# A first input tile in three column groups, and a burst of constant matmuls ahead of it

## The chip, the cores and the metric

The kernel runs on one core of a Trainium2 chip. The metric is the device time of one execution in microseconds; the figure given for a kernel is the median of several runs. Engines are named PE (matmul), ACT, DVE and POOL (element-wise work), and SP, which issues the DMAs here. Each engine works through its own list of instructions in order and meets the others only at semaphores.

## The reference

One step of a one-layer hybrid decoder: 1024 prompt rows and 8 sample rows of width 1024. What matters for the change is the head of it:

```
h = RMSNorm(x, g_pre)            # (1032, 1024)
z = h @ w_in                     # 1024 -> 2432 columns, split among three groups
u, v, ga, xb, gb, q, gc = split(z)
```

Group A is a chunked spatial gate on u and v, group B a short convolution and a gated linear recurrence, group C a cross attention into 256 memory rows. Their outputs are concatenated, multiplied with w_out, normalised and added to x. All of it is float32.

## The kernel before

**Layout.** x is kept transposed: 8 k-tiles of 128 features, each 128 partitions by 1032 columns (1024 prompt rows and 8 sample rows). The columns are worked on in NG = 3 groups of GN = 344. The input projection runs over 19 weight tiles of 128 outputs (m = 0 to 18), each of 8 k-tiles.

**Three products for one.** Each float32 product is made of three matmuls on rounded parts. ACT rounds a tile (x_hi, for x together with the factor g_pre; w_hi), DVE or POOL subtracts the rounded part from the whole (x_lo, w_lo), and `parts` (L358 to L364) multiplies w_hi with x_hi, w_hi with x_lo and w_lo with x_hi. So one k-tile of one weight tile is 9 matmuls, three for each column group. The norm's factor is applied later, on the results, since it is a factor per column; its sum of squares is made from the same tiles by ACT (L684) and DVE (L1042).

**The order at the start.** SP issues, all on one hardware queue (L255 to L262): the parameters, the first 256 columns of weight tile 0, k-tile 0 of x (L262), the rest of weight tile 0 (L259), k-tile 1, weight tile 1 (L246), k-tiles 2 to 7. Each load of a k-tile has a semaphore of its own (xT_in). ACT waits for each (L680), rounds it (L681) and counts xhi_done; DVE waits for that (L1037), makes x_lo (L1038) and counts xlo_done. ACT's and DVE's roundings and splits of weight tile 0 and 1 stand between those of k-tiles 0, 1 and 2 (L672, L677, L664; L1027).

PE's `start_tiles(m, k)` does the 9 matmuls of one k-tile for weight tile 0 or 1 and waits for the k-tile once, ahead of its first matmul. The opening order on PE is: tile 0 with k-tiles 0, 1, 2, then tile 1 with k-tile 0, tile 0 with k-tiles 3 and 4, and so on. Results of tiles 0 and 1 lie in PSUM banks 0 to 5. The tile `ones` (128x128), which POOL sets early (L922), is used on PE for the sum of squares over partitions (L407); PSUM bank 7 is first used there too.

**After the start.** ACT's rounding of weight tile 2 waits for the end of tile 0 on PE; behind it stand the rest of the squares, the sums on DVE, the memory projection and the reciprocal root, which PE waits for before the rest of tile 2 and 3.

Of the kernel before, what the change touches and what calls it, by code (L numbers as in the profile page):

```python
# [26 lines left out]
F = mybir.dt.float32  # L27
R = mybir.dt.float32r
ALU = mybir.AluOpType
ACT = mybir.ActivationFunctionType  # L30
AX = mybir.AxisListType

P = 128
# [3 lines left out]
KT = DM // P  # L37
NG = 3
GN = TT // NG
# [16 lines left out]
for _name, _n in (("g_pre", 8), ("g_mem", 8), ("w_conv", 12), ("b_conv", 3), ("b_a", 3), ("b_x", 3),  # L56
                  ("lam", 3), ("st_conv", 72), ("st_h", 24), ("b_s", 4)):
    PAR[_name] = _at
    _at += _n
N_PAR = _at  # L60

K_ORDER = [3, 4, 5, 6, 7, 0, 1, 2]
MIX_BANKS = (6, 7, 4)
# [24 lines left out]
def build(nc, d):  # L88
    with ExitStack() as ctx:
# [3 lines left out]
        def sem(name):  # L93
            return ctx.enter_context(nc.semaphore(name))

        x_hi, x_lo = sb("x_hi", [P, KT, TT], R), sb("x_lo", [P, KT, TT], R)
# [9 lines left out]
        ident, ones = sb("ident", [P, P]), sb("ones", [P, P])  # L106
# [12 lines left out]
        ps = ctx.enter_context(nc.psum_tensor("ps", [P, 8, 512], F))  # L119
# [58 lines left out]
        def wo_source(n):  # L178

            if n in (0, 1, 7):  # L180
                return w_stage[:, n % 7, :]
            return wo_early[:, n - 2, :] if n < 6 else zT[:, 0, 0:DM]

        def pc(name, i=0, n=1):
            return par[:, PAR[name] + i:PAR[name] + i + n]
# [3 lines left out]
            "par_in", "rows_in", "gatew_in", "wsT_in", "memn_in"))  # L189
        memT_in = [sem(f"memT_in{i}") for i in range(4)]  # L190
        wm_in = [sem(f"wm_in{i}") for i in range(4)]
        xT_in = [sem(f"xT_in{k}") for k in range(KT)]
        w_in = [sem(f"w_in{i}") for i in range(2)]
        x_in = [sem(f"x_in{i}") for i in range(2)]
        c_in = [sem(f"cache_in{i}") for i in range(6)]
        wo_in = [sem(f"wo_in{i}") for i in range(KT)]
        gpost_in = sem("gpost_in")
        y_stored = [sem(f"y_stored{i}") for i in range(2)]
        kv_stored, conv_stored, h_stored, vs_stored, ys_stored = map(sem, (
            "kv_stored", "conv_stored", "h_stored", "vs_stored", "ys_stored"))  # L200
        const_set, w_masked, wlo_done, qc_done, xsq_done, whi_done, xhi_done = map(sem, (
            "const_set", "w_masked", "wlo_done", "qc_done", "xsq_done", "whi_done", "xhi_done"))
        xlo_done, memg_done, ms_done, root_done, xsum_done, rstdB_done = map(sem, (
            "xlo_done", "memg_done", "ms_done", "root_done", "xsum_done", "rstdB_done"))
# [39 lines left out]
        def _(sp):  # L244
# [9 lines left out]

            sp.dma_start(par[:, :], d["par"]).then_inc(par_in, 16)  # L255
            sp.dma_start(w_stage[:, 0, 0:WF], d["w_tiles"][0, :, 0:WF]).then_inc(wfirst_in, 16)
            for k in range(KT):
                if k == 1:
                    sp.dma_start(w_stage[:, 0, WF:DM], d["w_tiles"][0, :, WF:DM]).then_inc(w_in[0], 16)  # L259
                if k == 2:  # L260
                    load_w(1, 1)
                sp.dma_start(mixT[:, k, :], d["xT"][:, k, :]).then_inc(xT_in[k], 16)  # L262
            sp.wait_ge(wlo_done, 1)
            load_w(2, 0)
            for i in range(4):
# [38 lines left out]
            sp.wait_ge(a_done, 9)  # L304

            def load_wo(n):
                sp.dma_start(wo_source(n), d["w_out"][K_ORDER[n]]).then_inc(wo_in[n], 16)

            for n in range(2, 6):
                load_wo(n)  # L310
# [46 lines left out]
        def _(pe):  # L357
            def parts(g, slot, k, cols, x, bank):  # L358

                wk = slice(k * P, (k + 1) * P)  # L360
                for n, (w, xx) in enumerate(((w_hi, x_hi), (w_hi, x_lo), (w_lo, x_hi))):
                    last = pe.matmul(ps[:, bank, 0:GN], w[:, slot, wk], xx[:, k, cols],  # L362
                                     start=(x == 0 and n == 0), stop=(x == KT - 1 and n == 2))
                return last  # L364
# [18 lines left out]
            def start_tiles(m, k):  # L383
                if m == 0 and k == 0:
                    pe.wait_ge(wfirstlo_done, 1)
                elif (m, k) in ((0, WF // P), (1, 0)):
                    pe.wait_ge(wlo_done, m + 1)
                if m == 0:
                    pe.wait_ge(xlo_done, k + 1)
                for g in range(NG):  # L390
                    last = parts(g, m, k, slice(g * GN, (g + 1) * GN), k, 3 * m + g)
                    if k == KT - 1:
                        last.then_inc(z_done, 1)

            for k in range(KT):
                start_tiles(0, k)
                if k in (2, 4, 6):
                    start_tiles(1, k // 2 - 1)
# [7 lines left out]
            for g in range(NG):  # L406
                pe.matmul(ps[:, 5 + g, 0:GN], ones[:, :], probs[:, g * GN:(g + 1) * GN],  # L407
                          start=True, stop=True).then_inc(rstdp_done, 1)
# [3 lines left out]
            for k in range(KT):  # L412
                pe.wait_ge(mlo_done, k // 2 + 1)
                pe.wait_ge(wmlo_done, k // 2 + 1)
                for mt in range(MT):
                    for n, (a, w) in enumerate(((memT_hi, w_mem_hi), (memT_lo, w_mem_hi),
                                                (memT_hi, w_mem_lo))):
                        last = pe.matmul(ps[:, 3 + mt, :], a[:, k, mt * P:(mt + 1) * P], w[:, k, :],
                                         start=(k == 0 and n == 0), stop=(k == KT - 1 and n == 2))
# [16 lines left out]
            with pe.Fori(0, 4) as i:  # L436
                for u in range(2):
                    m, s = i * 2 + (ATT0 + u), i * 2 + u
                    pe.wait_ge(qc_done, s * 2 + 2)
                    for t in range(2):  # L440
                        for hh in range(2):
# [4 lines left out]
                                             start=False, stop=True)  # L446
# [10 lines left out]
                    for h in range(NH):  # L457
                        if h % 2 == 0:
                            pe.wait_ge(pTlo_done, s * 2 + (h // 2 + 1))
                        for mt in range(MT):  # L460
                            pT = slice((2 * h + mt) * P, (2 * h + mt + 1) * P)
                            pe.matmul(ps[:, 7, h * 2 * HD:(h + 1) * 2 * HD], probsT_hi[:, pT], v_hl[:, mt, h, :],  # L462
                                      start=(mt == 0), stop=(mt == 1), skip_group_check=True)
# [171 lines left out]
            for x, k in enumerate(K_ORDER):  # L635
                for n in range(2):
                    cols = slice(n * 512, (n + 1) * 512)
                    pe.matmul(ps[0:2 * NL, 6 + n, :], o_s[:, k, :], wo_hi[:, k, cols],
                              start=(x == 0), stop=(x == KT - 1), skip_group_check=True)
                    last = pe.matmul(ps[0:NL, 6 + n, :], o_s[:, k, 0:NL], wo_lo[:, k, cols],  # L640
                                     start=False, stop=(x == KT - 1), skip_group_check=True)
# [14 lines left out]
        def _(act):  # L656
# [14 lines left out]
            act.wait_ge(wfirst_in, 16)  # L671
            act.activation(w_hi[:, 0, 0:WF], w_stage[:, 0, 0:WF], ACT.Copy).then_inc(wfirsthi_done, 1)  # L672
            act.wait_ge(par_in, 16)
            for k in range(KT):
                if k == 1:
                    act.wait_ge(w_in[0], 16)
                    act.activation(w_hi[:, 0, WF:DM], w_stage[:, 0, WF:DM], ACT.Copy).then_inc(whi_done, 1)  # L677
                if k == 2:
                    split_tile(1)
                act.wait_ge(xT_in[k], 16)  # L680
                act.activation(x_hi[:, k, :], mixT[:, k, :], ACT.Copy, scale=pc("g_pre", k)).then_inc(xhi_done, 1)  # L681
            for k in range(KT):
                act.wait_ge(xlo_done, k + 1)
                act.activation(mixT[:, k, :], mixT[:, k, :], ACT.Square).then_inc(xsq_done, 1)  # L684
                if k == 3:
                    split_tile(2)
# [182 lines left out]
            split_o(0, 1)  # L869

            for n, k in enumerate(K_ORDER):
                act.wait_ge(wo_in[n], 16)
                if n < KT - 1:
                    act.wait_ge(x_free, n + 1)
                else:
                    act.wait_ge(z_done, 3 * N_TILES)
                act.activation(wo_hi[:, k, 0:DM], wo_source(n), ACT.Copy).then_inc(wohi_done, 1)
# [127 lines left out]
        def _(dve):  # L1005
# [12 lines left out]
            def grp(g):  # L1018
                return slice(g * GN, (g + 1) * GN)
# [10 lines left out]
            dve.wait_ge(wfirsthi_done, 1)  # L1030
            low_w(0, slice(0, WF)).then_inc(wfirstlo_done, 1)

            for k in range(KT):
                if k in (1, 2):
                    dve.wait_ge(whi_done, k)
                    low_w(k - 1, slice(WF, DM) if k == 1 else slice(0, DM)).then_inc(wlo_done, 1)
                dve.wait_ge(xhi_done, k + 1)  # L1037
                dve.scalar_tensor_tensor(x_lo[:, k, :], mixT[:, k, :], pc("g_pre", k), x_hi[:, k, :].bitcast(F),  # L1038
                                         ALU.mult, ALU.subtract).then_inc(xlo_done, 1)
            for k in range(1, KT):  # L1040
# [215 lines left out]
            for g in range(NG):  # L1256
                evac(15, g, zT[:, 10, grp(g)])
                for c in range(3 * g, 3 * g + 3):
                    dve.wait_ge(mT_done, c + 1)
                    n, a = (P, 0) if c < NCH else (NS, P - NS)  # L1260
# [175 lines left out]
```

## Time and profile before

| | us |
|---|---|
| runs | 455.29, 454.79, 454.98 |
| median | 454.98 |
| span of the profiled execution | 450.6 |
| own time of the profiled execution | not recorded beyond its span |
| median less span | 4.4 |
| PE busy | 428.5 |
| DVE busy | 230.0 |
| ACT busy | 172.9 |
| POOL busy | 133.2 |

The span runs from the first to the last instruction of the profiled execution. Busy times are sums of instruction times; the ends of matmuls are modelled, so one matmul's time overlaps the next one's. Starts, and the step from one start to the next, are the surer readings.

### The profile page before, as it was taken

Reading aid. Unit: us, or ns where it says so; the run is one execution under the profiler, and the core shown is the slowest. Engines: PE = TensorE matmul, PEld = TensorE weight load, DVE = VectorE, ACT = ScalarE, POOL = GpSimd, SP = SyncE. Lnnn points to the kernel's source line nnn. Section 1 sums busy time; section 2 is a strip of 40 time slices with the busy share of each in tenths; the row PEclk is TensorE's granted clock in tenths of the full one; section 3 lists DMA queues with packets and bytes.
Section 4 is the critical chain, followed back from the end, with each engine's and each line's share of the span. In section 5 each row is a group of like instructions: output and inputs, shape, how many; then the busy total and the mean of one; then the engine's idle time right before and its main releaser. Section 6 shows DMA issues by size and latency. Waiting matters only on the chain.

```text
span 450.6 us, 6211 instructions
## 1 busy us (share of the span) xinstructions
PE 428.5 (95%) x2452; PEld 375.7 (83%) x2452; DVE 230.0 (51%) x325; ACT 172.9 (38%) x284; POOL 133.2 (30%) x71
## 2 busy tenths in 40 slices
PE   2999979999999999999999879999999999999994
PEld 2999878999999999998889577887899768888883
DVE  4978898333476674334359933265465634111112
ACT  5963655232232232225482330743725432222211
POOL 0024812132142232112039820410502323444440
PEclk9999999999999999999999969999999999999998
DMA  8990010111011111011042410132215320222222
GB/s 294 384 412 21 31 64 9 41 47 47 0 47 49 49 47 47 0 47 48 0 153 81 140 49 1 47 125 109 63 36 153 93 94 0 93 93 93 93 97 93
DMA packets 12916, 38.18 MB, mean 85 GB/s; under 512 B 2096, under 2 KB 2488, under 8 KB 12768
## 3 DMA queue, kind: packets, MB, share of 16 engines
q1 hardware_dynamic: 12896, 37.91, 24.2%
q8 instruction: 13, 0.21, 0.2%
q14 instruction: 7, 0.06, 0.0%
HBM read 33.07 MB, written 4.83 MB: 84 GB/s over the span
## 4 chain that ended last, share of the span: by engine, by line
PE 80%; DVE 11%; ACT 3%; issue 3%; DMA 2%; SPq 1%; DVEq 0%; ACTq 0%
PE ps L362 40%; PE ps L627 20%; PE ps L491 2%; PE ps L486 2%; PE ps L445 2%; PE ps L462 2%; PE ps L444 2%; DMA mixT<-in_xT 2%; PE ps L453 2%; PE ps L561 1%; PE ps L539 1%; DVE zT L1224 1%; DVE probs L1042 1%; DVE memT_lo L1057 1%; PE ps L464 1%
## 5 line engine op out<-in xcount | busy, mean ns | idle before, releaser
L362 PE MATMUL ps<-x_hi,w_hi 128*128 128x344 f32 x456 | 152.2, 334 | 11.4 <-DVE x_lo L1038 8.9
L362 PE MATMUL ps<-x_hi,w_lo 128*128 128x344 f32 x456 | 146.9, 322 | 0.0
L362 PE MATMUL ps<-x_lo,w_hi 128*128 128x344 f32 x456 | 146.8, 322 | 0.0
L362 PEld LDWEIGHTS ps<-x_hi,w_hi 128*128 128x128 f32 x456 | 87.1, 191 | 15.4 <-issue 14.3
L914 POOL TENSOR_TENSOR w_lo<-w_stage,w_hi 128x1024 fp32r<-128x1024 f32 x17 | 40.7, 2392 | 173.2 <-ACT w_hi L664 173.2
L362 PEld LDWEIGHTS ps<-x_lo,w_hi 128*128 128x128 f32 x456 | 87.0, 191 | 0.1
L362 PEld LDWEIGHTS ps<-x_hi,w_lo 128*128 128x128 f32 x456 | 86.8, 190 | 0.0
L627 PE MATMUL ps<-x_hi,w_hi 128*128 128x512 f32 x128 | 50.6, 395 | 0.0
L627 PE MATMUL ps<-x_hi,w_lo 128*128 128x512 f32 x128 | 50.5, 394 | 0.0
L627 PE MATMUL ps<-x_lo,w_hi 128*128 128x512 f32 x128 | 50.5, 394 | 0.0
L664 ACT ACTIVATE w_hi<-w_stage 128x1024 fp32r<-128x1024 f32 x18 | 19.0, 1054 | 69.0 <-PE ps L362 68.9
L1011 DVE TENSOR_TENSOR zT<-ps,rstdB 128x344 f32<-128x344 f32 (+1 forms) x27 | 13.8, 513 | 46.1 <-PE ps L362 46.1
L987 POOL TENSOR_TENSOR zT<-zT,x_ring 128x1024 f32<-128x1024 f32 x7 | 16.8, 2396 | 42.5 <-DVE zT L1323 42.5
L627 PEld LDWEIGHTS ps<-x_hi,w_lo 128*128 128x128 f32 x128 | 24.1, 188 | 5.7
L627 PEld LDWEIGHTS ps<-x_hi,w_hi 128*128 128x128 f32 x128 | 24.0, 188 | 5.7
L627 PEld LDWEIGHTS ps<-x_lo,w_hi 128*128 128x128 f32 x128 | 24.0, 188 | 5.7
L1318 DVE TENSOR_SCALAR sy<-sy 128x1 f32<-128x1 f32 x7 | 1.1, 154 | 54.2 <-ACT probs L860 54.2
L944 POOL TENSOR_TENSOR q_st<-zT,q_st 64x256 fp32r<-64x256 f32 x16 | 14.0, 875 | 45.7 <-ACT q_st L716 44.3
L860 ACT ACTIVATE probs<-ps 128x1024 f32<-128x1024 f32 x7 | 7.2, 1025 | 51.9 <-PE ps L627 51.9
L979 POOL TENSOR_TENSOR w_lo<-mixT,w_hi 128x1024 fp32r<-128x1024 f32 x8 | 19.2, 2398 | 21.2 <-ACT w_hi L852 21.2
L738 ACT ACTIVATE probs<-ps,negm 128x256 f32<-128x256 f32 x32 | 14.7, 473 | 18.8 <-DVE negm L1117 18.8
L1011 DVE TENSOR_TENSOR mixT<-ps,rstdB 128x344 f32<-128x344 f32 x15 | 7.4, 514 | 24.1 <-PE ps L362 24.0
(196 smaller groups left out, 662.4 us busy)
## 6 DMA issues: line engine op xcount, KB each, us to landing
w_stage<-in_w_tiles SPq DMA_DIRECT2D x18, 512.0 KB, 3.3
mixT<-in_xT SPq DMA_DIRECT2D x8, 516.0 KB, 7.9
x_ring<-in_x_all SPq DMA_DIRECT2D x8, 512.0 KB, 4.0
o_y<-zT SPq DMA_DIRECT2D x7, 512.0 KB, 2.9
zT<-in_w_out SPq DMA_DIRECT2D x5, 512.0 KB, 4.6
zT<-in_w_mem SPq DMA_DIRECT2D x4, 512.0 KB, 12.6
zT<-in_kcT SPq DMA_DIRECT2D x8, 256.0 KB, 4.1
zT<-in_vc SPq DMA_DIRECT2D x8, 256.0 KB, 6.1
```

What stands on the lines that cost most here:

```text
L362: last = pe.matmul(ps[:, bank, 0:GN], w[:, slot, wk], xx[:, k, cols], start=(x == 0 and n == 0), stop=(x == KT - 1 and n == 2))
L444: pe.matmul(out, q_st[:, u, hh, t, :], k_hh[:, hh, t, :], start=True, stop=False)
L445: last = pe.matmul(out, q_st[rows_h, u, hh, t, :], k_lo[rows_h, t, :], start=False, stop=True)
L453: last = pe.transpose(ps[:, 5 + b, n * P:(n + 1) * P], probs[:, (4 * b + n) * P:(4 * b + n + 1) * P], ident[:, :])
L627: last = pe.matmul(ps[:, 3 * u + n, :], o[:, u, ok], w[:, k, cols], start=(x == 0 and part == 0), stop=(x == KT - 1 and part == 2))
L664: act.activation(w_hi[:, slot, :], w_stage[:, slot, :], ACT.Copy).then_inc(whi_done, 1)
L738: act.activation(probs[:, h * NM:(h + 1) * NM], ps[:, 3 + hh, t * NM:(t + 1) * NM], ACT.Exp, bias=negm[:, n:n + 1], scale=HD ** -0.5, accu ...
L914: pool.tensor_tensor(w_lo[:, slot, :], w_stage[:, slot, :], w_hi[:, slot, :].bitcast(F), ALU.subtract).then_inc(wlo_done, 1)
L944: pool.tensor_tensor(q_st[to, u, hh, :, :], zT[r, 0:2, bass.ds(i * (2 * P) + u * P, P)], q_st[r, u, hh, :, :].bitcast(F), ALU.subtract).th ...
L979: pool.tensor_tensor(o_lo[:, slot, :].rearrange("p (k n) -> p k n", k=KT), mixT[:, :, bass.ds(c0, P)], o_hi[:, slot, :].bitcast(F).rearran ...
L987: pool.tensor_tensor(y_out[:, u, :], y_out[:, u, :], x_ring[:, u, 0:DM], ALU.add).then_inc(y_ready, 1)
L1011: dve.tensor_tensor(dst, ps[:, g, 0:GN], rstdB[:, g * GN:(g + 1) * GN], ALU.mult).then_inc(z_used, 1)
```

## The change

The load, the rounding and the splitting of k-tile 0 are each done in three column groups of 344, with a semaphore for each group (x0_in, x0hi_done, x0lo_done), and PE waits for each group before the three matmuls of that group. Before its first such wait PE does WARM = 22 matmuls of `ones` with `ones` (128 columns, float32) into PSUM bank 7, which is written again later by L407; nothing reads the burst's results. k-tiles 1 to 7 are moved as before, and their semaphores (now ktile_in) are used a second time for the eight tiles of w_out, which had eight of their own.

```diff
+WARM = 22
@@ semaphores @@
-        xT_in = [sem(f"xT_in{k}") for k in range(KT)]
+        ktile_in = [sem(f"ktile_in{k}") for k in range(KT)]
-        wo_in = [sem(f"wo_in{i}") for i in range(KT)]
+        x0_in = [sem(f"x0_in{g}") for g in range(NG)]
+        x0hi_done, x0lo_done = sem("x0hi_done"), sem("x0lo_done")
@@ SP @@
-            for k in range(KT):
+            for g in range(NG):
+                cols = slice(g * GN, (g + 1) * GN)
+                sp.dma_start(mixT[:, 0, cols], d["xT"][:, 0, cols]).then_inc(x0_in[g], 16)
+            for k in range(1, KT):
...
-                sp.dma_start(mixT[:, k, :], d["xT"][:, k, :]).then_inc(xT_in[k], 16)
+                sp.dma_start(mixT[:, k, :], d["xT"][:, k, :]).then_inc(ktile_in[k], 16)
@@ PE @@
-                if m == 0:
-                    pe.wait_ge(xlo_done, k + 1)
+                if m == 0 and k > 0:
+                    pe.wait_ge(xlo_done, k)
                 for g in range(NG):
+                    if m == 0 and k == 0:
+                        pe.wait_ge(x0lo_done, g + 1)
                     last = parts(g, m, k, slice(g * GN, (g + 1) * GN), k, 3 * m + g)
...
+            pe.wait_ge(const_set, 4)
+            for _ in range(WARM):
+                pe.matmul(ps[:, 7, 0:P], ones[:, :], ones[:, :], start=True, stop=True)
@@ ACT @@
-            for k in range(KT):
+            for g in range(NG):
+                cols = slice(g * GN, (g + 1) * GN)
+                act.wait_ge(x0_in[g], 16)
+                act.activation(x_hi[:, 0, cols], mixT[:, 0, cols], ACT.Copy, scale=pc("g_pre", 0)).then_inc(x0hi_done, 1)
+            for k in range(1, KT):
...
             for k in range(KT):
-                act.wait_ge(xlo_done, k + 1)
+                act.wait_ge(xlo_done if k else x0lo_done, k if k else NG)
...
-                act.wait_ge(wo_in[n], 16)
+                act.wait_ge(ktile_in[n], 32 if n else 16)
@@ DVE @@
-            for k in range(KT):
+            for g in range(NG):
+                dve.wait_ge(x0hi_done, g + 1)
+                dve.scalar_tensor_tensor(x_lo[:, 0, grp(g)], mixT[:, 0, grp(g)], pc("g_pre", 0),
+                                         x_hi[:, 0, grp(g)].bitcast(F), ALU.mult, ALU.subtract).then_inc(x0lo_done, 1)
+            for k in range(1, KT):
...
-                dve.wait_ge(xhi_done, k + 1)
+                dve.wait_ge(xhi_done, k)
```

On PE, at the opening of the program, stood (one row is one instruction; in brackets what it waits for):

```order
L362 MATMUL ps<-x_hi,w_hi 128x344 [waits xlo_done,wfirstlo_done]
L362 MATMUL ps<-x_lo,w_hi 128x344
L362 MATMUL ps<-x_hi,w_lo 128x344
L362 MATMUL ps<-x_hi,w_hi 128x344
L362 MATMUL ps<-x_lo,w_hi 128x344
L362 MATMUL ps<-x_hi,w_lo 128x344
```

and now stands there:

```order
L405 MATMUL ps<-ones 128x128 [waits const_set]
L405 MATMUL ps<-ones 128x128 x21
L368 MATMUL ps<-x_hi,w_hi 128x344 [waits x0lo_done,wfirstlo_done]
L368 MATMUL ps<-x_lo,w_hi 128x344
L368 MATMUL ps<-x_hi,w_lo 128x344
L368 MATMUL ps<-x_hi,w_hi 128x344 [waits x0lo_done]
```

The burst stands ahead of the first wait for x, and that wait is now one for each column group.

On ACT, from the rounding of weight tile 0's first columns to that of k-tile 2, stood:

```order
L672 ACTIVATE w_hi<-w_stage 128x256 [waits wfirst_in]
L681 ACTIVATE x_hi<-mixT,par 128x1032 [waits xT_in0,par_in]
L677 ACTIVATE w_hi<-w_stage 128x768 [waits w_in0]
L681 ACTIVATE x_hi<-mixT,par 128x1032 [waits xT_in1]
L664 ACTIVATE w_hi<-w_stage 128x1024 [waits w_in1]
L681 ACTIVATE x_hi<-mixT,par 128x1032 [waits xT_in2]
```

and now stands there:

```order
L683 ACTIVATE w_hi<-w_stage 128x256 [waits wfirst_in]
L688 ACTIVATE x_hi<-mixT,par 128x344 [waits x0_in0,par_in]
L688 ACTIVATE x_hi<-mixT,par 128x344 [waits x0_in1]
L688 ACTIVATE x_hi<-mixT,par 128x344 [waits x0_in2]
L692 ACTIVATE w_hi<-w_stage 128x768 [waits w_in0]
L696 ACTIVATE x_hi<-mixT,par 128x1032 [waits ktile_in1]
L675 ACTIVATE w_hi<-w_stage 128x1024 [waits w_in1]
L696 ACTIVATE x_hi<-mixT,par 128x1032 [waits ktile_in2]
```

One instruction has become three; the order around it, and up to k-tile 2, is the same. DVE's list and SP's change in the same way.

## Rows read from the trace of the kernel before

**Rows 1.** The page, part 1: PE's busy time, share of the span, instructions.

```profile
PE 428.5 (95%) x2452; PEld 375.7 (83%) x2452; DVE 230.0 (51%) x325; ACT 172.9 (38%) x284; POOL 133.2 (30%) x71
```

**Rows 2.** Waits of PE: who waited for whom, us in total, times, longest.

```profile
PE ps L362 <- DVE x_lo L1038: 8.9, 2, 8.5
PE ps L561 <- DVE zT L1246: 4.7, 1, 4.7
PE ps L362 <- DVE mixT L1011: 2.5, 1, 2.5
```

**Rows 3.** Timeline of the opening: start us, us, engine, line, what [idle before].

```profile
1.56 0.20 POOL L922 MEMSET ones<- 128x128 f32 x1
...
5.92 1.15 ACT L681 ACTIVATE x_hi<-mixT,par 128x1032 fp32r<-128x1032 f32 x1 [1.72 <-DMA mixT<-in_xT]
6.98 0.83 ACT L677 ACTIVATE w_hi<-w_stage 128x768 fp32r<-128x768 f32 x1
7.11 1.29 DVE L1038 SCALAR_TENSOR_TENSOR x_lo<-mixT,par,x_hi 128x1032 fp32r<-128x1032 f32 x1 [2.45 <-ACT x_hi L681]
8.11 1.16 ACT L681 ACTIVATE x_hi<-mixT,par 128x1032 fp32r<-128x1032 f32 x1 [0.30 <-DMA mixT<-in_xT]
...
8.54 0.63 PE L362 MATMUL ps<-x_hi,w_hi 128*128 128x344 f32 x1 [8.54 <-DVE x_lo L1038]
```

**Rows 4.** The chain of waits, opening: start us, us, what.

```profile
1.74 0.42 SPq L262
...
3.63 7.02 DMA mixT<-in_xT
...
10.67 1.17 ACT x_hi L681
...
11.86 1.30 DVE x_lo L1038
...
13.30 13.00 PE ps L362 x81
...
26.39 1.06 ACT w_hi L664
```

**Rows 5.** Busy time by stretch: PE, PEld, DVE, ACT, POOL, granted clock, DMA, GB/s.

```profile
3.00:4.00 1.00, 0.00 (x0) 0.00 (x0) 0.16 (x1) 0.42 (x2) 0.00 (x0) 1.00 0.71 168
8.00:11.00 3.00, 2.46 (x9) 2.49 (x10) 2.97 (x4) 2.55 (x3) 0.00 (x0) 1.00 1.03 420
29.40:30.20 0.80, 0.80 (x7) 0.80 (x6) 0.80 (x1) 0.80 (x1) 0.62 (x1) 1.00 1.01 381
...
8.50:11.26 2.76, 2.71 (x9) 2.75 (x10) 2.73 (x3) 2.42 (x3) 0.00 (x0) 1.00 1.02 419
...
50.00:60.00 10.00, 7.63 (x33) 5.82 (x31) 8.83 (x7) 3.03 (x5) 6.97 (x4) 1.00 0.31 106
...
257.10:261.76 4.66, 0.00 (x0) 0.03 (x1) 4.59 (x8) 1.90 (x3) 4.66 (x3) 0.87 0.72 258
261.76:267.40 5.64, 5.64 (x22) 5.64 (x23) 0.88 (x2) 2.21 (x4) 0.34 (x1) 0.50 0.01 2
```

**Rows 6.** DMA packets in 2.4 to 3.1, then in 29.4 to 30.2 us.

```profile
DMA packets 129, 0.14 MB, mean 199 GB/s; under 512 B 13, under 2 KB 122, under 8 KB 129
...
DMA packets 172, 0.30 MB, mean 381 GB/s; under 512 B 22, under 2 KB 125, under 8 KB 170
```

**Rows 7.** Timeline of PE, full float32 matmuls (L561) at either clock.

```profile
252.29 2.02 PE L561 MATMUL ps<-zT,wsT 128*128 128x96 f32 x16
254.16 0.77 PE L486 MATMUL ps<-mixT,gate_w 128*128 128x344 f32 x2
...
261.76 2.00 PE L561 MATMUL ps<-zT,wsT 128*128 128x96 f32 x8 [4.67 <-DVE zT L1246]
263.46 0.63 PE L362 MATMUL ps<-x_hi,w_hi 128*128 128x344 f32 x1
```

**Rows 8.** Groups of ACT by form: busy us, mean ns, idle before.

```profile
L761 ACT ACTIVATE zT<-ps,par 128x344 f32<-128x344 f32 x9 | 4.9, 548 | 25.4 <-PE ps L491 20.0 <-DVE probsT L1207 5.4
```

More of the change, by code:

```diff
@@ L306, in load_wo @@
             def load_wo(n):
-                sp.dma_start(wo_source(n), d["w_out"][K_ORDER[n]]).then_inc(wo_in[n], 16)
+                sp.dma_start(wo_source(n), d["w_out"][K_ORDER[n]]).then_inc(ktile_in[n], 16)
             for n in range(2, 6):
@@ L679, in _ @@
                     split_tile(1)
-                act.wait_ge(xT_in[k], 16)
+                act.wait_ge(ktile_in[k], 16)
                 act.activation(x_hi[:, k, :], mixT[:, k, :], ACT.Copy, scale=pc("g_pre", k)).then_inc(xhi_done, 1)
             for k in range(KT):
-                act.wait_ge(xlo_done, k + 1)
+                act.wait_ge(xlo_done if k else x0lo_done, k if k else NG)
                 act.activation(mixT[:, k, :], mixT[:, k, :], ACT.Square).then_inc(xsq_done, 1)
```

## The prediction

> **What bounds the kernel now.** I read the page first: PE is busy 95% of a span of 450.6 us, so only time in which PE stands still, or work on PE itself, can be worth much [rows 1]. The list of PE's waits then says where it stands still: 8.9 us in two waits for x_lo at the start, 4.7 us in one wait for a DVE result (it lies at 257 us), 2.5 us before 60 us [rows 2]. The change is at the first of them, so I read the opening as a timeline [rows 3] and looked at what the chain that ended last passes through there [rows 4].
>
> The reader is to see two things. PE's first matmul starts at 8.54 because k-tile 0 of x is rounded (ACT 5.92, 1.15 us) and split (DVE 7.11, 1.29 us) in whole pieces. But the chain does not pass through that matmul. It goes from the issue of k-tile 2 of x at 3.63 over 7.02 us of DMA to its rounding at 10.67, its split at 11.86 and only then to PE at 13.30 [rows 4]. PE did the 18 matmuls of k-tiles 0 and 1 from 8.54 on and then stood still for 0.4 us, the second of its two waits (8.9 in all, the longest 8.5), until x_lo of k-tile 2 was there [rows 2, 3]. From 13.30 PE runs without a gap to 26.3, where tile 0's end lets ACT round weight tile 2, and from there the chain runs on [rows 4]. So what counts is when PE can start on k-tile 2, not when it starts at all.
>
> **The change, part by part.** The profiled execution has a span of 450.6 us; the median of the runs is 454.98. The record gives no own time for that execution beyond its span, so I take the difference, 4.4 us, as what lies around the span, and the sum is made on the span.
>
> *Earlier start of k-tile 0.* Before, landing at 5.9 (ACT starts at 5.92), then 2.6 us to PE. With three pieces ACT's first piece is at most 0.55 us (a 344-column ACTIVATE out of PSUM [rows 8]) and DVE's about 1.29 / 3 = 0.43 [rows 3]: PE could have its first piece about a microsecond after the first third has landed, between 5 and 6 us. The three ACT pieces take at most 3 x 0.55 = 1.65 in place of 1.15, but two of them run while the last piece is still on its way; if that lands at 6.2, ACT is done by 6.8. Its next tile of x lands only at 8.11 (it waits for DMA there), and between them is one weight rounding of 0.83 [rows 3], so the extra half microsecond is hidden. What this frees is PE time before 13.30, of which PE already had 0.4 too much. Worth to the end: 0.
>
> *The burst.* 22 matmuls of a 128x128 constant in full float32. The kernel's other full float32 matmuls, L561 (four heads of 96 columns), leave two records each: 16 records from 252.29 to 254.16, 0.117 us each at 2.4 GHz, and 8 records from 261.76 to 263.46, 0.213 us each at a granted clock of 0.50, which is 1.2 GHz [rows 7]. So the burst is 44 records. It can start when the ones tile is set, at 1.76 [rows 3]. All at 1.2 GHz it ends at 1.8 + 9.4 = 11.2. But the clock will rise in it. The granted-clock column reads 1.00 at the start and is no help, the step is: the first matmuls of 344 columns run 9 in the 2.7 us from 8.54 to 11.26 [rows 5], 0.3 us each, after that 0.16 each (81 in 13.0 us [rows 4]). PE had worked 2.7 us when it rose there, and 5.6 us (261.76 to 267.40) the other time [rows 5]. With these the burst ends at 4.5 + 31 x 0.117 = 8.2, or at 7.4 + 18 x 0.117 = 9.5. If 128 columns cost 128/96 of 96, that is 0.28 and 0.156 us, the second becomes 7.4 + 24 x 0.156 = 11.2. I take 8.2 to 9.5, since at the other clock 0.117 is no less than 128 columns would need by the step of the 344-column matmuls (0.16 x 128 / 344 = 0.06 for one pass, two passes a record). Queued behind it on PE are the 18 matmuls of k-tiles 0 and 1, 18 x 0.16 = 2.9 us; so nothing is lost if the burst ends before 13.3 - 2.9 = 10.4. Nobody else waits for PE that early: its first result is asked for at tile 0's end. Worth: 0, with the 4.4 us of slack to 13.3 as cover. The 1.1 us that full speed saves on k-tile 0 falls into the same slack.
>
> *The DMA in three pieces.* This is the only part on the chain. SP issues two DMAs more ahead of everything else, 2 x 0.47 us (from the issue of k-tile 0 at 1.74 to that of k-tile 2 at 3.63 there are four [rows 4]). k-tile 2's issue moves from 3.63 to about 4.6, but its bytes only flow after those before it: 16 DMA engines are already full (share 1.03 from 8 to 11 us [rows 5]) and 2.2 MB stand ahead of it (k-tiles 0 and 1, weight tiles 0 and 1, parameters). So the issue time is hidden by the backlog. What isn't hidden is the time of the packets: one row of a tile is one packet, 4128 bytes before, three of 1376 now, 384 packets and not 128 for the tile. Long packets move at 420 GB/s from 8 to 11 us [rows 5], 26.2 bytes per ns and engine, 157 ns for one of 4128 bytes. In the stretch 29.4 to 30.2, where 103 of 150 packets (without those under 512 bytes) are rows of 1568 bytes, the rate is 381 GB/s at about the same share [rows 5, 6]. Solving for the small ones: (0.8 x 16 x 1.01 - 0.14 MB at 26.2) / 103 = 74 ns each, 65 ns if it goes by size. 24 small packets per engine are then 1.56 to 1.78 us against 8 x 0.157 = 1.26: +0.3 to +0.5. The dear end: from 2.4 to 3.1 us, where the queue has just begun, 116 packets of about 1 KB took 0.7 x 16 / 116 = 0.10 us each [rows 6]: 24 x 0.10 - 1.26 = +1.1. The other end is a gain: from 3 to 4 us the engines moved 168 GB/s [rows 5], so 0.6 us of full rate was lost there on long rows; if short pieces fill that, k-tile 2 lands 0.6 us earlier, and ACT and DVE would follow, since each waits for data there. I take +0.3, by the stretch at 29.4, which is the nearest in size and in load.
>
> The Trainium skill (DMA: Bandwidth & Descriptors, Specifications) states that line rate wants transfers of 512 bytes and more; 1376 is above that, and by it this term is nought and the time would be 455.0. The trace bears it out only partly: rows of 1568 bytes moved at 381 where long ones moved at 420.
>
> *Renamed semaphores* for x's tiles and the output weights: the same waits, 0.
>
> Sum: 450.6 + 0 + 0 + 0.3 + 4.4 = **455.3 us**. PE starts k-tile 2 at about 13.6.
>
> **Rivals.**
> *A. The slow stretch after 257 us moves (faster).* PE stands still from 257.10 to 261.76, the clock falls, and after the restart PE works 5.64 us at 1.2 GHz [rows 5]. At the start it needed only 2.7. If the burst or the shift changes where the clock rises, up to 2.9 us of slow work become fast. A slow step is (267.40 - 263.46) / 14 = 0.28 us, 22 records less the 8 of L561 [rows 5, 7], a fast one 0.16: 2.9 x (1 - 0.16/0.28) = 1.2 us, 454.1. If the clock does not fall at all: 5.64 x 0.43 = 2.4, 452.9. For it: the two rises differ by 2.9 us with nothing in the program to explain it. Against it: three runs agree within 0.5 us, so the place is the same each time, and nothing near 257 us is edited.
> The Trainium skill (TensorE: Matmul & The Clock Gate, What's actually happening) says the activity monitor runs free and does not restart with a kernel, and that the point of the rise varies from run to run. By that rule a shift is luck and the three runs should differ by more than they do; the trace does not bear it out, but three runs can't exclude it.
> *B. The burst is too long (slower).* Place: the 44 records ahead of k-tile 0 on PE. If the clock does not rise under them they end at 11.2, and the 18 matmuls behind them start at 1.2 GHz: 2.7 us for nine, then nine at 0.16, 1.4 us: 15.3 for k-tile 2, +2.0 us, 457.0. If it does rise but late, with the dearer step: 11.2 + 2.9 = 14.1, +0.8, 455.8. It decides from a burst end of 10.4. For it: the restart at 261.76 began with just such matmuls and took 5.6 us to speed up. Against it: even 5.6 us leave a margin of 0.9.
> *C. Short packets are dear:* +1.1, 456.1.
> *D. Short pieces fill the DMA's start:* -0.6, 454.4.
> *E. The clock falls while PE waits.* PE now has pauses of about 1.3 us before k-tiles 1 and 2. If it fell, 2.7 to 5.6 us would run slow, +1.2 to +2.4, 456.5 to 457.7. Against it: a pause of 2.5 us at 57 to 60 us [rows 2] left the clock at 1.00 from 50 to 60 [rows 5].
> *F. The earlier start carries through.* It would need k-tile 2 not to be the gate. With the burst over at 8.2 and 2.9 us for k-tiles 0 and 1, k-tile 2 could start at 11.1, 2.2 us earlier: 452.8. Against it stands the chain: PE waits there for a DVE result that waits for ACT and DMA.
>
> **How the numbers follow.** The forecast 0.62, A 0.17, B 0.10, C 0.04, D 0.04, E 0.02, F 0.01. A change of 0.2%, 0.9 us, is what a measurement of this kernel can tell from none. Faster: A and F, 0.18. Slower: B without its mild half, C, E and a little of the upper packet prices, 0.15. Within: 0.67. The likeliest case by itself spans 454.8 to 455.8. The range goes down to 453.6, which takes in A's milder half, and up to 457.0, which takes in C and B.
>
> **What would show it.** In the profile after, the first records of PE near 1.8; the burst over by 9.5; the first 344-column matmuls already 0.16 us apart; x_hi of k-tile 0 in three, PE's wait for x_lo split over k-tiles 1 and 2; the first matmul of k-tile 2 within 13.3 to 13.8. The DMA term is right if the rounding of k-tile 2 starts at 10.8 to 11.2. The forecast is wrong if that rounding starts before 10.4, if k-tile 2's first matmul comes right behind k-tile 1's last without a wait (B), or if the stretch at granted clock 0.50 after 257 us has another length than 5.6 us (A).

## The result, and the profile after

The changed kernel takes 455.59 us (median of 20 runs, 454.14 to 457.3), the kernel before 454.44 in the same comparison (20 runs, 452.25 to 455.29). The ratio is 1.0034, 95% interval [1.0021, 1.0047]: slower by 0.34%, or 1.5 us (the two medians as they stand differ by 1.15). The time lies inside the forecast range, 0.3 us above the forecast, but the likeliest class, no change within 0.2%, was missed on the slow side.

One thing about the basis first. The profiled execution of the changed kernel took 454.48 us with a span of 452.8: 1.7 us lie around the span, and 1.7 to 1.8 in the profiled run of every other kernel below (2.1 in e10). The profile before, with its span of 450.6, must then be of an execution of about 452.3, one of the fastest of that kernel, and not of its median. The 4.4 us of the prediction stood for 1.7.

The opening of the changed kernel as a timeline (start us, us, engine, line, operation, what [idle before]), the counterpart of [rows 3]:

```profile
1.74 1.37 SPq L262 DMA_DIRECT2D mixT<-in_xT  x3
1.82 7.28 PE L405 MATMUL ps<-ones 128*128 128x128 f32 x44 [1.82 <-POOL ones L937]
4.54 1.05 ACT L688 ACTIVATE x_hi<-mixT,par 128x344 fp32r<-128x344 f32 x2 [0.29 <-DMA mixT<-in_xT]
6.66 0.58 ACT L688 ACTIVATE x_hi<-mixT,par 128x344 fp32r<-128x344 f32 x1 [1.07 <-DMA mixT<-in_xT]
8.86 0.40 PE L368 MATMUL ps<-x_hi,w_hi 128*128 128x344 f32 x1
9.10 0.31 PE L368 MATMUL ps<-x_lo,w_hi 128*128 128x344 f32 x1
...
12.65 0.43 PE L368 MATMUL ps<-x_hi,w_hi 128*128 128x344 f32 x1 [2.14 <-DVE x_lo L1057]
12.65 2.46 ACT L696 ACTIVATE x_hi<-mixT,par 128x1032 fp32r<-128x1032 f32 x2 [0.23 <-DMA mixT<-in_xT]
```

The split works as the diff says: two thirds of k-tile 0 are rounded from 4.54 on, where the whole tile was rounded from 5.92 on [rows 3]. The burst runs from 1.82 to about 8.9 and PE meets k-tile 0 at full speed. But k-tile 0's first matmul starts at 8.86 (before 8.54), because the burst stands ahead of it; k-tile 1's comes at 12.65 (before 11.26), 2.14 us after PE has run out; and the rounding of k-tile 2 starts at 12.65, where it was 10.67.

The chain of waits there (start us, us, what), the counterpart of [rows 4]:

```profile
3.63 6.46 DMA mixT<-in_xT
10.11 1.17 ACT x_hi L696
...
11.30 1.30 DVE x_lo L1057
...
12.65 2.61 PE ps L368 x9
15.28 13.56 PE ps L368 x81
28.93 1.06 ACT w_hi L675
```

It now passes through k-tile 1. Its landing is late, and the nine matmuls of k-tile 1 last 2.6 us, because the clock falls at 13.1, under the third of them. k-tile 2's data are split late too, so PE starts on them at 15.28 where it started at 13.30, and the 81 matmuls from there to the end of tile 0 take 13.56 us where they took 13.00 [rows 4]. That is +2.0 and +0.5, 2.5 us at the end of tile 0.

PE's waits (who waited for whom, us in total, times, longest), the counterpart of [rows 2]:

```profile
PE ps L572 <- DVE zT L1265: 4.7, 1, 4.7
PE ps L368 <- DVE mixT L1026: 2.5, 1, 2.5
PE ps L368 <- DVE x_lo L1057: 2.1, 1, 2.1
PE ps L405 <- POOL ones L937: 1.8, 1, 1.8
```

The 8.9 us of waiting for x_lo have shrunk to 2.1 and 1.8 for the constant, and the kernel is slower: time in which PE waited became time in which PE multiplied a constant.

Busy time by stretch (PE, PEld, DVE, ACT, POOL, granted clock, DMA share, GB/s), of the changed kernel:

```profile
5.00:7.00 2.00, 2.00 (x14) 2.00 (x14) 1.06 (x2) 0.93 (x3) 0.00 (x0) 1.00 0.84 232
13.10:16.50 3.40, 3.38 (x12) 2.97 (x12) 3.28 (x4) 3.02 (x3) 0.00 (x0) 0.50 1.02 415
259.60:264.30 4.70, 0.06 (x2) 0.00 (x0) 4.63 (x8) 1.87 (x3) 4.70 (x3) 0.78 0.74 260
```

and of the kernel before, one stretch that was not read for the prediction:

```profile
5.00:7.00 2.00, 0.00 (x0) 0.00 (x0) 0.00 (x0) 1.08 (x2) 0.00 (x0) 1.00 1.01 403
```

Two things happen. From 5 to 7 us, behind and under the small pieces, the DMA engines move 232 GB/s, not 403. And from 13.1 to 16.5 us, just after PE's wait, the granted clock is 0.50, which is 1.2 GHz; in the trace before there is no such stretch at this place. From 20 us to 255 us the two profiles stand 2.5 to 2.6 us apart, and at the end 2.2 (the spans: 452.8 and 450.6). The 0.4 us between come from the stretch behind the wait at 257 us: PE restarts at 264.34 in place of 261.76, but works at 1.2 GHz only to 269.2, 4.9 us and not 5.6.

### The profile page after: what moved, and what is told of

Its sections match the earlier page's. It is cut to its first block, busy times and chain, and to the rows that moved or that the text cites. A ratio compares the mean times of both kernels' runs of the same rounds, so it can differ in the third digit from the quotient of the medians.

```text
span 452.8 us, 6305 instructions
## 1 busy us (share of the span) xinstructions
PE 435.6 (96%) x2496; PEld 382.3 (84%) x2496; DVE 230.3 (51%) x327; ACT 173.4 (38%) x286; POOL 133.5 (29%) x71
## 4 chain that ended last, share of the span: by engine, by line
PE 80%; DVE 11%; ACT 3%; issue 3%; DMA 1%; SPq 1%; DVEq 0%; ACTq 0%
PE ps L368 41%; PE ps L638 20%; PE ps L502 2%; PE ps L497 2%; PE ps L456 2%; PE ps L473 2%; PE ps L455 2%; PE ps L464 1%; PE ps L572 1%; PE ps L550 1%; DMA mixT<-in_xT 1%; DVE zT L1243 1%; DVE probs L1061 1%; DVE memT_lo L1076 1%; PE ps L475 1%
## 5 line engine op out<-in xcount | busy, mean ns | idle before, releaser
L1002 POOL TENSOR_TENSOR zT<-zT,x_ring 128x1024 f32<-128x1024 f32 x7 | 16.8, 2397 | 42.6 <-DVE zT L1342 42.6
```

Source lines behind the costliest of these rows:

```text
L1002: pool.tensor_tensor(y_out[:, u, :], y_out[:, u, :], x_ring[:, u, 0:DM], ALU.add).then_inc(y_ready, 1)
```

## The experiments

"Against before" is the ratio to the kernel before, run on the same chip; e1 to e4, e5 to e8 and e9 to e12 had a chip each. Its own executions spread from 452.3 to 455.5 us there, so single times say little and the starts in the trace say more.

### Which part costs: the burst taken out, the burst alone, the transfer whole, the transfer alone

**e1_pieces_no_burst**, of the changed kernel:

```diff
-WARM = 22
+WARM = 0
```

> The changed kernel with WARM = 0: k-tile 0 moved, rounded and split in three, no burst. Theory T (transfer): the three short-row transfers alone make k-tile 2 late, so its rounding on ACT starts at about 12.6 us as in the changed kernel (before 10.7), PE's first matmul at about 6 to 8.5 and at 1.2 GHz, and the time is about 1.0034 of before, since PE's early work is hidden anyway. Theory B (burst): the burst is what disturbs the transfers or the clock; then k-tile 2's rounding starts near 10.7 and the ratio is 1.000.

Measured: 455.77 us median, 1.0040 [1.0022, 1.0058]. The chain of this kernel (start us, us, what):

```profile
12.48 17.05 PE ps L368 x90
```

Without the burst k-tile 1 still starts at 12.48, and k-tile 2's rounding at 12.50. So the burst's matmuls don't delay the data. PE starts k-tile 0 at 5.80 but then pauses 3.3 us, and the step from one matmul to the next falls from 0.29 to 0.16 us, the sign of the higher clock, only at 18.2: 17.05 us for 90 matmuls, where 13.00 + 9 x 0.16 = 14.4 would do at full speed. Tile 0 ends at 29.53, 0.7 us later than with the burst.

**e2_burst_only**, of the kernel before:

```diff
+            pe.wait_ge(const_set, 4)
+            for _ in range(22):
+                pe.matmul(ps[:, 7, 0:P], ones[:, :], ones[:, :], start=True, stop=True)
```

> The kernel before with the burst of 22 matmuls alone; k-tile 0 whole. Theory T: k-tile 2's rounding starts at 10.7 as before, PE's first 344-column matmul at about 9.1 (burst end), k-tile 2's at 13.3, ratio 1.000 (0.999 to 1.001). Theory B: rounding of k-tile 2 later than 11.5, or the clock falls within 10 to 16 us, ratio above 1.002.

Measured: 453.08 us, 0.9982 [0.9967, 0.9996]. Its chain:

```profile
10.85 1.17 ACT x_hi L684
...
13.48 13.02 PE ps L362 x81
```

The burst costs nothing on this chain: 13.48 against 13.30, by a landing that is 0.2 later. The 0.2% by which this one came out faster is dealt with at e10.

**e3_whole_dma**, of the changed kernel (rounding, split and matmuls of k-tile 0 stay in three, the burst stays):

```diff
-            for g in range(NG):
-                cols = slice(g * GN, (g + 1) * GN)
-                sp.dma_start(mixT[:, 0, cols], d["xT"][:, 0, cols]).then_inc(x0_in[g], 16)
+            sp.dma_start(mixT[:, 0, :], d["xT"][:, 0, :]).then_inc(x0_in[0], 16)
...
-                act.wait_ge(x0_in[g], 16)
+                act.wait_ge(x0_in[0], 16)
```

> The changed kernel with k-tile 0 moved by one transfer of whole rows; rounding, splitting and PE's waits stay in three, the burst stays. Theory T: k-tile 2's rounding starts at 10.7, k-tile 2's first matmul at 13.3, no fall of the clock before 17 us, ratio 1.000. Theory B: as the changed kernel, ratio 1.003.

Measured: 453.72 us, 0.9989 [0.9972, 1.0006]. Its chain:

```profile
10.69 1.17 ACT x_hi L694
...
13.32 13.00 PE ps L366 x81
```

**e4_dma_pieces_only**, of the kernel before (only the transfer in three; ACT waits for all of them):

```diff
-                sp.dma_start(mixT[:, k, :], d["xT"][:, k, :]).then_inc(xT_in[k], 16)
+                for cols in ([slice(g * GN, (g + 1) * GN) for g in range(NG)] if k == 0 else [slice(0, TT)]):
+                    sp.dma_start(mixT[:, k, cols], d["xT"][:, k, cols]).then_inc(xT_in[k], 16)
...
-                act.wait_ge(xT_in[k], 16)
+                act.wait_ge(xT_in[k], 16 if k else 48)
```

> The kernel before with only the transfer of k-tile 0 in three column groups; rounding and splitting whole, no burst. Theory T: k-tile 2's rounding at 12.6, PE's first matmul at about 9.3 (k-tile 0 lands at 6.6), span about 2.0 us longer, ratio 1.003 to 1.0045. Theory B: rounding at 10.7 to 11.1, ratio 1.000 to 1.001.

Measured: 455.39 us, 1.0024 [1.0012, 1.0036]. Its chain:

```profile
4.58 7.91 DMA mixT<-in_xT
12.52 1.17 ACT x_hi L682
...
15.15 13.00 PE ps L363 x81
```

The four agree. The start of k-tile 2's rounding is 12.50 and 12.52 where the transfer is in three (e1, e4), 10.85 and 10.69 where it is whole (e2, e3), 10.67 before, 12.65 after. Later runs repeat it: 12.69 and 12.70 in e7 and e9 with three, 10.93 and 10.76 in e8 and e10 with one. The transfer alone makes this delay; everything else in the change is 0 within 0.2 us at 13.3. And e4 shows that it is not the burst that disturbs the DMA. At the end of tile 0 e4 is 1.85 us behind and the changed kernel 2.5: most of what the transfer alone does not make is the fall of the clock at 13.1, which e4's trace does not have. In time e4 came out at +0.24%, a little under the 0.3 to 0.45% expected.

### Short rows or many transfers

**e5_one_dma_short_rows**: the kernel before, one transfer for k-tile 0, but from a copy of it in memory in which each third of a row is padded (1408 bytes apart), so that no piece can be longer than 1376 bytes.

```diff
+                if k == 0:
+                    sp.dma_start(mixT[:, 0, :].rearrange("p (g n) -> p g n", g=NG), d["x0p"][:, :, 0:GN]).then_inc(xT_in[0], 16)
```

**e6_three_dmas_long_rows**: the kernel before, k-tile 0 in three transfers by partitions (0:48, 48:96, 96:128), rows of 4128 bytes.

> The kernel before, k-tile 0 still one transfer and one issue, but read from a copy of it in DRAM laid out as three padded groups a row, so that it moves as 384 packets of 1376 bytes in place of 128 of 4128. Theory S (size of the packets): k-tile 2's rounding starts at about 12.5 us and k-tile 2's first matmul at 15.1, as with three short transfers; ratio about 1.003 to 1.004. Theory N (number of transfers, their issue and their start): the rounding starts at 10.7 to 11.2, ratio 1.000 to 1.001.

> The kernel before, k-tile 0 moved by three transfers, cut by partitions (48, 48, 32) so that each row is still one packet of 4128 bytes. Theory S: rounding of k-tile 2 at 10.7 to 11.0, ratio 1.000. Theory N: at about 12.5, ratio 1.003 to 1.004.

Measured: e5 454.46 us, 1.0001 [0.9986, 1.0017]; e6 455.24 us, 1.0017 [0.9999, 1.0035]. Timeline of ACT in e5, then the stretch from 5 to 7 us:

```profile
11.60 3.74 ACT L684 ACTIVATE x_hi<-mixT,par 128x1032 fp32r<-128x1032 f32 x3 [0.22 <-DMA mixT<-in_xT]
...
5.00:7.00 2.00, 0.00 (x0) 0.00 (x0) 0.00 (x0) 0.55 (x1) 0.00 (x0) 1.00 1.02 337
```

and in e6:

```profile
13.10 2.43 ACT L682 ACTIVATE x_hi<-mixT,par 128x1032 fp32r<-128x1032 f32 x2 [0.23 <-DMA mixT<-in_xT]
...
5.00:7.00 2.00, 0.00 (x0) 0.00 (x0) 0.00 (x0) 0.37 (x1) 0.00 (x0) 1.00 0.84 150
```

Short rows alone put k-tile 2's rounding at 11.60, +0.9 us, between what the two theories expected; three transfers of long rows put it at 13.10, +2.4 us, beyond both. The two don't add up (0.9 + 2.4 is more than the 2.0 of both together), and e6 also cuts the tile another way than the change does, so its 2.4 is not a term of the change. From 6 to 7 us, before, in e5 and in e6:

```profile
6.00:7.00 1.00, 0.00 (x0) 0.00 (x0) 0.00 (x0) 1.00 (x2) 0.00 (x0) 1.00 1.02 417
6.00:7.00 1.00, 0.00 (x0) 0.00 (x0) 0.00 (x0) 0.55 (x1) 0.00 (x0) 1.00 1.00 325
6.00:7.00 1.00, 0.00 (x0) 0.00 (x0) 0.00 (x0) 0.37 (x1) 0.00 (x0) 1.00 0.75 169
```

In this microsecond no row of 1376 bytes lands any more in e5: the traces count 85 packets of over 2 KB there, 52 in e6 and 105 before, and else only such under 512 bytes. Share of engine time over long packets gives an estimate of at most 0.19 us each in e5 and 0.23 in e6, where it was 0.155. So the loss is only in part a price of the short packets and of idle engines; the long packets behind the cut tile, of the transfers that follow, took longer too. Why is not shown, and e5 also reads from a copy with another layout in memory, which was not tried apart.

The times are weaker than the traces here. e5's 1.0001 does not show the 0.9 us (0.2%), and its interval ends just short of it. e6's 1.0017 is 0.8 us, while its profiled execution ended tile 0 3.5 us late, since PE's clock rose there only at 18.2. Four of e6's ten executions had the same mean granted clock as the profiled one, 0.99, and spans of 451.8, 451.9, 453.7 and 454.0: the 2.4 us are read from the slowest of them and may not be typical.

### The clock

**e7_after_filler**: the changed kernel, with more constant matmuls in PE's wait for k-tile 1 (`fill(n, bank)` does n matmuls of `ones` with `ones` into a PSUM bank).

```diff
+                if k == 0:
+                    fill(8, 7)
```

> The changed kernel with 8 more matmuls of the constant between k-tile 0's and k-tile 1's, in the 2.1 us in which PE waits for x_lo. If the fall of the clock at 13.1 us comes from that pause: no stretch at granted clock 0.50 before 50 us, k-tile 2's first matmul still at 15.3, tile 0's 81 matmuls from there in 13.0 in place of 13.56 us, so 0.5 us less at 28 us. If the fall has another cause: a stretch at 0.50 in 10 to 17 us again.

Measured: 455.35 us, 1.0021 [1.0003, 1.0038]. By stretch:

```profile
10.50:13.10 2.60, 2.60 (x23) 2.59 (x22) 1.94 (x3) 2.26 (x3) 0.00 (x0) 1.00 1.02 411
13.10:16.50 3.40, 2.43 (x15) 2.17 (x15) 3.28 (x4) 3.06 (x3) 0.00 (x0) 1.00 1.02 416
```

With PE kept busy the clock stays up from 13.1 to 16.5, where it was 0.50 in the changed kernel, and tile 0 ends at 28.34, not 28.84: the fall there cost 0.5 us. The total is too coarse to show it: 1.0021 against 1.0034, with intervals that overlap. The mean granted clock of all executions speaks for it as well: in none of the 20 of the changed kernel is it above 0.986, in four of the ten of e7 it is 0.989 or 0.990, with spans of 452.1 to 452.8, the four shortest of e7.

In the profiled execution of e7 the clock fell at 62.0 us instead, behind the 2.5 us wait for mixT. That wait is in every kernel without fillers for it; the clock fell behind it in the profiled executions of e2, e3, e4, e5 and e7, and not in those of before, after, e1 and e6. The stretches of e2:

```profile
57.50:60.25 2.75, 0.33 (x2) 0.00 (x0) 2.71 (x4) 0.52 (x1) 0.00 (x0) 0.95 0.55 191
60.30:63.70 3.40, 3.37 (x13) 3.40 (x14) 3.33 (x7) 1.68 (x4) 0.00 (x0) 0.55 0.02 5
```

and of before over nearly the same time:

```profile
60.10:63.70 3.60, 3.58 (x23) 3.60 (x24) 3.50 (x8) 1.86 (x5) 0.00 (x0) 1.00 0.00 0
```

13 matmuls in one, 23 in the other. Set against the trace before, e2 is 0.2 us behind at 60 us and 1.6 at 66 us, e3 0.0 and 1.6. So one such fall costs 1.4 to 1.5 us, and whether it comes differs between executions.

The record has span and mean granted clock of 81 executions of the kernel before. In 14 the clock is 0.989 or 0.990, as in the trace before, and the spans are 450.6 to 451.6; in the other 67 it is 0.983 to 0.987, and the spans are 451.4 to 453.7. A stretch of 3.4 us at half the clock would take 3.4 x 0.5 / 450 = 0.004 from the mean, so the trace before, without a fall at 60 us, is of the rarer kind. That these 67 had their fall at that place is an inference; that it takes a good part of the spread is as strong as that.

**e8_later_fillers**: the kernel before, with constant matmuls in the two later waits only, at 57 us and at 257 us.

```diff
+            pe.wait_ge(ms_done, 3)
+            fill(9, 7)
...
+                if g == 0:
+                    pe.wait_ge(z_used, 41)
+                    fill(20, 1)
```

> The kernel before with constant matmuls in PE's two later pauses: 9 in the 2.5 us before 60 us and 20 in the 4.7 us at 257 us. If the difference of 1.4 us that some executions show from 60 to 64 us and the slow stretch after 262 us are the clock falling in a pause: no stretch at 0.50 at 60 to 64 or after 261 us, 2.0 to 2.5 us gained at 262 us and up to 1.4 at 60 us, ratio 0.992 to 0.996, and runs closer together. If constant matmuls do not hold the clock: ratio 1.000.

Measured: 450.03 us (449.82 to 454.75, 12 runs), 0.9923 [0.9902, 0.9944]. By stretch:

```profile
57.50:60.30 2.80, 2.41 (x20) 2.17 (x18) 2.76 (x4) 0.48 (x1) 0.00 (x0) 1.00 0.54 187
...
257.20:262.00 4.80, 4.80 (x43) 4.42 (x40) 4.73 (x8) 2.18 (x4) 4.80 (x3) 1.00 0.69 261
262.00:268.00 6.00, 6.00 (x46) 6.00 (x46) 1.59 (x4) 2.28 (x4) 0.44 (x1) 1.00 0.01 3
```

46 records after 262 us in 6.0 us, where the kernel before did 22 in 5.64 [rows 5] (the two counts are not of the same matmuls). The data that PE waits for come no earlier; the work behind the waits runs at full speed. Eleven of the 12 times lie within 0.9 us, 449.82 to 450.65. Against the trace before, which has no fall at 60 us, the span is 2.3 us shorter (448.3); against the median of its runs, of which most seem to have such a fall (1.4 to 1.5 us), the time is 4.3 us shorter.

**e9_change_with_fillers**: the change and the fillers of e8 together.

> The changed kernel plus the constant matmuls in PE's two later pauses (9 before 60 us, 20 at 257 us), so that only the opening can differ from the kernel before with the same. If the change costs the opening and nothing else: 2.0 us more than the kernel before with fillers (450.0), 2.5 where the clock falls at 13 us: 452.0 to 452.5. If the cost is in how the clock falls later: 450.0 to 450.5.

Measured: 451.83 us (451.44 to 453.6, 7 runs), 0.9954 [0.9938, 0.9971]. Against e8 that is +1.8 us, or 1.4 by the two ratios, since e8 ran on another chip; e10, below, ran on the same chip as e9 and is 1.9 us shorter. So the change's own price, read where the later falls are gone, is 1.4 to 1.9 us, a little under the 2.0 to 2.5 expected. Its chain, and the stretch behind the wait for k-tile 1:

```profile
4.57 8.10 DMA mixT<-in_xT
12.70 1.17 ACT x_hi L705
...
14.10:17.50 3.40, 3.13 (x13) 2.72 (x12) 3.40 (x3) 3.15 (x3) 0.00 (x0) 0.60 1.02 414
```

The same rounding at 12.70, and the same fall, from 13.4 to 16.8.

### What the burst is worth, and the best version

**e10_fillers_burst**: e8 with a burst of 20 ahead of k-tile 0, transfer whole.

> The kernel before with the fillers in the two later pauses and a burst of 20 at the start, k-tile 0 whole. If the burst is worth nothing because k-tile 2 is the gate: 450.0, k-tile 2's first matmul at 13.3. If the gain of 0.18% that the burst alone showed is real and not the later clock: 449.2.

Measured: 449.92 us (449.88 to 450.17), 0.9907 [0.989, 0.9924]. Its chain:

```profile
10.76 1.17 ACT x_hi L693
...
13.40 6.70 PE ps L362 x41
```

0.1 us from e8 in time, on another chip; by the ratios 0.16%, with intervals that overlap. k-tile 2's first matmul starts at 13.40, in e8 at 13.56 and before at 13.30, so with k-tile 2's landing as the gate no worth of the burst is to be seen. e2's 0.2% was then not the burst's work on the chain. Five of e2's twelve executions have a mean granted clock of 0.989 or 0.990, and 9 of the 34 of the kernel before beside it: more of the better kind by chance is a likely cause, but it is not shown.

**e11_fillers_reorder** and **e12_fillers_burst_reorder**: weight tile 1 is moved behind k-tile 2 of x on SP, ACT and DVE, so that k-tile 2 lands earlier; e12 has the burst of 20 as well.

```diff
-                if k == 2:
+                if k == 3:
...
-                if k in (1, 2):
+                if k in (1, 3):
```

(The first pair stands on SP, at the load of weight tile 1, and on ACT, at its rounding; the second on DVE, at its low part.)

> The kernel before with the fillers, and weight tile 1 moved, rounded and split behind k-tile 2 and not ahead of it. If k-tile 2's data is the gate, its rounding starts 1.25 us earlier, at 9.4; PE's 18 cold matmuls then are the gate and k-tile 2 starts at 12.7, 0.6 us earlier: 449.4. If the gate is elsewhere: 450.0.

> Fillers, a burst of 20 at the start, k-tile 0 whole, and weight tile 1 behind k-tile 2. Now PE's cold start is gone and the data come 1.25 us earlier: k-tile 2 starts at 12.0 to 12.1, 1.2 us earlier than before, 448.8. Here the burst should be worth 0.6 us, which it was not while k-tile 2 gated. If it is worth nothing here either: 449.4 as without it.

Measured: e11 450.21 us (449.08 to 450.54), 0.9906 [0.9886, 0.9925]; e12 448.86 us (448.77 to 449.1), 0.9885 [0.9868, 0.9902]. The chain of e11, then two records of PE in it:

```profile
8.57 7.46 PE ps L362 x29
...
13.87 0.49 PE L362 MATMUL ps<-x_hi,w_hi 128*128 128x344 f32 x1
14.44 0.32 PE L362 MATMUL ps<-x_hi,w_lo 128*128 128x344 f32 x1
```

and the chain of e12:

```profile
6.29 1.16 ACT x_hi L693
7.48 1.29 DVE x_lo L1050
8.77 0.87 DVE w_lo L1039
9.64 1.29 DVE x_lo L1050
10.97 14.43 PE ps L362 x90
25.49 1.06 ACT w_hi L676
```

My expectation for e11 (k-tile 2 at 12.7) missed: the data were there at 11.9, but PE, at 1.2 GHz from 8.57, saw its clock rise only at 14.4, after 5.8 us of work, so k-tile 2 began at 13.87 and the gate was PE's own speed. In e12 the burst removes that: k-tile 1 starts at 10.97, 90 matmuls run through in 14.43, tile 0 ends at 25.40. The burst is worth 1.35 us here, against 0.6 expected and 0.1 in e10; since the rise came late in e11's profiled execution and earlier in others (2.7 us before, 3.1 in e8), part of the 1.35 is how late the clock rises without a burst. e12 beats the kernel before by 1.15%, and the changed kernel stands above that one.

## Why the prediction was right and wrong

**The gate: right.** It said that k-tile 2's landing decides and not PE's first matmul. After a start of k-tile 0 at 5.80 (e1), 8.74 (e2), 9.00 (e3) and 9.02 (e4) the rounding of k-tile 2 began at 12.50, 10.85, 10.69 and 12.52: the one does not follow the other. In the changed kernel k-tile 1 is late by the same transfer and delays PE besides.

**The burst: right.** 44 records from 1.82 to about 9 (8.2 to 9.5 forecast), worth 0 in its place (e2, e10). Rival B did not occur; PE was waiting again at 10.51. The prediction's "4.4 us of slack to 13.3" does not follow from its own numbers: with a burst end of 8.2 to 9.5 and a limit of 10.4 the slack was 0.9 to 2.2 us. Once k-tile 0 is moved in three, the burst is worth 0.7 us at the end of tile 0 (e1), which the medians, 455.77 and 455.59, do not resolve.

**The DMA in three pieces: right in place and sign, wrong in size.** This is the step that failed: "I take +0.3". k-tile 2's rounding, forecast for 10.8 to 11.2, came at 12.65: +2.0, with e4 alone +1.85. The term was mis-sized twice. Short rows cost 0.9 (e5) and not 0.3: nearer to the +1.1 from the first packets of the queue (rival C) than to the +0.3 to 0.5 from 29.4 us. The choice of the row "nearest in size and in load" took a loaded moment for what is a start of the queue; and the loss was not in the short packets alone, as the prediction had it, but in the long ones behind them as well. The number of transfers was priced by its issue time alone, 2 x 0.47 us, and that held to be hidden; one execution with three transfers of long rows says up to 2.4. The upper end, +1.1, was therefore no bound: no row showed a tile cut over several transfers at the start, and I should have said that the price was open upwards.
The rule of the Trainium skill (DMA: Bandwidth & Descriptors, Specifications) that made this term nought, full rate from 512 bytes on, is not borne out here: with k-tile 0 in rows of 1376 bytes (e5) the rounding of k-tile 2 came 0.9 us later, and from 5 to 7 us the engines moved 337 GB/s, fully busy, where with rows of 4128 bytes they moved 403 before and 373 in e3.

**Rival E: occurred, and was argued away on one execution.** The clock did fall, at 13.1, 0.45 us after a wait of PE of 2.14 us had ended, and stayed down for 3.4 us. I gave it 0.02 because the 2.5 us wait at 57 us had left the clock at 1.00 [rows 2, 5]. In five other profiled executions the clock fell behind that same wait. One trace that shows no fall is a draw, not a rule. Its price was smaller than either of my figures: 0.5 us (e7 against after), since most of the slow stretch lies before 15.28, where PE would have waited for k-tile 2 in any case. The record's mean clocks, read above, say that the one trace was of the rarer kind.
The Trainium skill (TensorE: Matmul & The Clock Gate, What's actually happening) says that the monitor runs free and that the point of the rise varies from run to run. I weighed that against three runs and took it as not borne out. The same opening agrees with it: the rise came 2.7 us after PE's start before, 3.1 in e8 and 5.8 in e11. Of falls the sentence says nothing; that they vary too, as at 60 us, the traces here show.

**The slow stretch after 257 us (rival A)** changed a little: PE restarted at 264.34, 2.6 us later, and the clock rose at 269.2, 1.8 later, so 4.9 us of work were slow and not 5.6, which gave back 0.4 us, under the 1.2 of A's milder half. e2, with k-tile 0 whole, has 4.9 us there too (263.25 to 268.2), so the cut tile is not what shortened it. The other price was near: 2.4 us were put down for no fall at all, and e8, which has none there, has a span 2.3 us shorter than before.

**The basis.** 4.4 us around the span was a difference between a fast execution and a median of others; the figure that fits is 1.7. Added to the span, the 4.4 only gives back the median of the three runs, 454.98, and that lies 0.5 us above the 454.44 of twenty runs. Had the basis been 454.44, the same working would have given 454.7, against 455.59 measured. That the forecast lies 0.3 us off is thus no merit of the sum: of the change it said +0.3, and it is +1.5 by the ratio and 1.4 to 1.9 where the later falls are gone. A basis 0.5 us too high stood in for part of a term that was too small, and that is luck.

## What to carry to other kernels

Cut a transfer at the head of a kernel only if the chain passes through that tile; here it passed through a tile further back in the same queue, and that one paid for the cut. A warming burst is worth nothing while data are the gate and more once they are not (0.1 against 1.35 us here), so first bring the data forward, then warm. And read the granted clock behind each of TensorE's waits, in more than one execution: filling the two later waits with a constant multiplication gave 0.8%, more than anything at the start of the kernel.

## What the hardware showed that was not expected

- Three transfers for one tile, with rows as long as before, delayed what was behind them in the queue by 2.4 us in the one execution profiled (e6), more than their issue time. The engines were busy 0.84 of the time from 5 to 7 us and moved 150 GB/s (403 with one transfer), and the long packets of the transfers behind took about 0.23 us each from 6 to 7 us, not 0.155. The cause stays open.
- The same wait of 2.5 us let the clock fall in five profiled executions and not in four others, the fall costing 1.4 to 1.5 us. A wait of 2.1 us (the changed kernel) was followed by one too; the wait of 4.7 us at 257 was followed by one in each of these nine.
- The first rise of the clock came 2.7 us after PE had begun to work without a pause (e8: 3.1), but 5.8 us after in e11. In e1, where PE had begun at 5.80 and paused 3.3 us, it came at 18.2, 5.7 us after the restart. In the burst it came between 3.7 us (e2) and 5.7 us (e7) after the start, seen by the step of its records, which falls from about 0.2 to about 0.11 us; so multiplications of ones by ones raise it too. In all these the granted-clock column reads 1.00 up to the rise.
